# The expert loop of a mixture-of-experts layer, written as a pipeline over blocks

## What is computed

```python
scores = sigmoid(u @ router_w); _, idx = top_k(scores + router_b, 8)      # 128 experts
wts = s_sel / sum(s_sel) * 2.5
# the 4096 (token, expert) pairs, sorted by expert, cut in blocks of one expert each
def group_fn(xg, e):                     # xg: the rows of one block
    g, up = split(xg @ w_gu[e], 2)       # w_gu[e]: 1024 x 512, 2 MB
    return (silu(g) * up) @ w_down[e]    # w_down[e]: 256 x 1024, 1 MB
out = zeros.at[row_tok].add(y * row_w)   # each row is added to its token's sum
```

## Time and profile before

| | us |
|---|---|
| three runs | 1600.34, 1602.52, 1602.64 |
| median | 1602.52 |
| the profiled execution, span from its first to its last instruction | 1598.8 |
| first silu of the expert loop to its last (70 of them) | 742.3 to 1555.5 |

### The profile page before, as it was taken

The page is one execution under the profiler, slowest core; times in us unless marked ns, Lnnn a source line. Parts: engine busy times, 40 slices in busy tenths (PEclk is TensorE's granted clock), DMA queues, the critical chain, the costliest instruction groups (busy, mean ns, idle before and its releaser), DMA issues.

```text
span 1598.8 us, 26750 instructions
## 1 busy us (share of the span) xinstructions
PE 1357.2 (85%) x5742; PEld 975.4 (61%) x5743; DVE 939.1 (59%) x1838; ACT 635.9 (40%) x878; POOL 247.8 (15%) x311
## 2 busy tenths in 40 slices
PE   1699996779999978866989999898899998898990
PEld 0288874568888757534656666666566666565660
DVE  4713338968225876535776576776757556455544
ACT  1363225333213312224555354564555454334432
POOL 0000000000000000002222322323223223232320
PEclk9999998889999989887999999999999999999995
DMA  9412201133225856136999888998989888778743
GB/s 304 133 53 87 72 0 53 53 118 117 94 93 189 284 161 210 66 145 222 329 308 270 243 266 244 329 330 255 315 268 320 243 268 237 213 224 228 218 89 118
DMA packets 111191, 310.59 MB, mean 194 GB/s; under 512 B 16217, under 2 KB 19489, under 8 KB 110898
## 3 DMA queue, kind: packets, MB, share of 16 engines
q1 hardware_dynamic: 82176, 241.20, 43.8%
q0 software_dynamic: 20592, 54.03, 16.1%
q10 hardware_dynamic: 8386, 14.89, 2.6%
...
...
## 4 chain that ended last, share of the span: by engine, by line
PE 42%; DMA 22%; DVE 14%; issue 8%; ACT 6%; ACTq 4%; DVEq 2%; POOLq 1%; POOL 1%; SPq 0%
PE psum L1300 23%; DMA expert_sum<-y_rows,add_idx 12%; PE psum L1467 6%; PE psum L1484 4%; DMA xg<-u_rows,row_idx 4%; DMA gu_raw<-in_exp_w_gu 4%; PE psum L1275 4%; ACT gu_hi L800 2%; DVE tmp_tok L964 2%; ACT y_rows L823 1%; DVE gu_lo L1215 1%; PE psum L1367 1%; PE psum L1358 1%; POOL step_word L547 1%; PE psum L1474 1%
## 5 line engine op out<-in xcount | busy, mean ns | idle before, releaser
L1215 DVE TENSOR_TENSOR gu_lo<-gu_raw,gu_hi 128x1024 f32 x212 | 246.8, 1221 | 112.6 <-ACT gu_hi L800 112.4
L1484 PE MATMUL psum<-w_dn,mask 128*128 x560 | 260.4, 608 | 36.9 <-DVE mask L1235 36.9
L800 ACT ACTIVATE gu_hi<-gu_raw 128x1024 f32 x212 | 209.8, 1048 | 112.7 <-issue 76.4
L1467 PE MATMUL psum<-gu_hi,xT_hi 128*128 x560 | 240.6, 430 | 8.8 <-DVE xT_lo L1205 5.0
L1467 PE MATMUL psum<-gu_hi,xT_lo 128*128 x560 | 219.7, 392 | 0.0
L1467 PE MATMUL psum<-gu_lo,xT_hi 128*128 x560 | 219.1, 391 | 0.0
L1484 PEld LDWEIGHTS psum<-w_dn,mask 128*128 128x128 f32 x560 | 101.2, 190 | 144.6 <-issue 144.6
L400 DVE TENSOR_TENSOR w_lo<-ring,w_hi 128x1024 fp32r<-128x1024 f32 x80 | 95.2, 1223 | 94.5 <-ACT w_hi L393 92.4
L1300 PE MATMUL psum<-uT_hi,w_hi 128*128 128x512 f32 x352 | 138.7, 394 | 13.3 <-DVE w_lo L400 12.2
L823 ACT ACTIVATE y_rows<-psum,row_w 128x512 f32<-128x512 f32 x140 | 88.5, 682 | 147.2 <-DMA expert_sum<-y_rows,add_idx 140.9
L1467 PEld LDWEIGHTS psum<-gu_hi,xT_hi 128*128 128x128 f32 x560 | 105.7, 189 | 56.0 <-issue 36.2
...
## 6 DMA issues: line engine op xcount, KB each, us to landing
...
mods<-in_x ACTq DMA_DIRECT2D x1, 2048.0 KB, 13.0
```

Of the source, the lines that this page charges most:

```text
L800: act.activation(gu_hi[:, bass.ds(order % 2, 1), PK * p:PK * p + PK].rearrange("p o k f -> p (o k) f"), gu_raw[:, PK * p:PK * p + PK], ACT ...
L1215: tt(gu_lo[at].rearrange("p o k f -> p (o k) f"), gu_raw[:, PK * p:PK * p + PK], gu_hi[at].rearrange("p o k f -> p (o k) f").bitcast(F32), ...
L1467: mm = pe.matmul(moe_bank(GU), rows[:, k], w[:, gu_place, k].rearrange("p o n -> p (o n)"), start=(k == 0 and n == 0), stop=(k == KT - 1 a ...
L1484: mm = pe.matmul(moe_bank(Y0 + g), hT[:, j], w_dn[:, place, j, g * NC:(g + 1) * NC].rearrange("p o n -> p (o n)"), start=(j == 0), stop=(j ...
```

## The change

The loop body now holds four blocks. PE makes gate/up of block `b+1` before down of block `b`; down weights and `hT` are split in two parts like the others, so down is twelve `fp32r` matmuls in place of four float32 ones. The three weight tiles hold a whole expert: `ew_raw` (one place), `ew_hi` and `ew_lo` (two places), each loaded and split in three pieces of 1 MB (two of gate/up, one of down). `xT_hi`, `xT_lo` and `y_rows` have two places each, `xg` has two instead of three. A gather is issued three blocks ahead instead of two. ACT may write `y_rows` of `b` once the addition of `b-2` has landed; the additions themselves are still one at a time. The pick is one comparison over 512 columns with `rel` worked out first, instead of four over 128. Ahead of the loop POOL stores the empty row block to the sum twice instead of once.

```diff
-UNROLL, SPAN = 3, 6
+UNROLL, SPAN = 4, 4
+AHEAD = 3
+HALVES = 3
...
             # SP, for each fresh block
-                    for p in range(PIECES):
-                        if not first:
-                            sp.wait_ge(gu_split, order * PIECES + p + 1)
-                        sp.dma_start(gu_raw[:, PK * p:PK * p + PK], ...).then_inc(gu_in[p], 16)
-                load_gu(b + UNROLL)
-                load_down(b + UNROLL, s, 2 * b + 4)
+                    for p in range(HALVES):
+                        sp.wait_ge(ew_split, order * HALVES + p + 1)
+                        sp.dma_start(ew_raw_of(p), ew_source(e, p)).then_inc(ew_in[p], 16)
...
             # POOL, block b
-                pool.wait_ge(xT_psum, 2 * b + 2)
-                gather(b + 2, (s + 2) % UNROLL, 2 * b + 2)
-                pool.wait_ge(scattered, 16 * b + 16)
-                pool.wait_ge(y_ready, 2 * b + 4)
+                pool.wait_ge(xT_psum, b + 2)
+                gather(b + AHEAD, (s + AHEAD) % UNROLL, 2 * b + 3)
+                pool.wait_ge(scattered, 16 * b + 32)
+                pool.wait_ge(y_ready, b + 2)
...
             # ACT, block b (after)
+                act.wait_ge(hT_psum, b + 1)
+                act.activation(hT_hi[:]..., moe_bank(HT)[:, 0:2 * P], ACT.Copy).then_inc(hT_hi_ready, 1)
+                rows_hi(b + 2, s)
+                expert_hi(b + 1, (2,))
+                expert_hi(b + 2, (0,))
+                silu(b + 1)
+                expert_hi(b + 2, (1,))
+                act.wait_ge(idx_ready, b + 1)
+                act.wait_ge(scattered, 16 * b + 16)
+                act.wait_ge(y_psum, b + 1)
+                act.activation(y_rows[:, s % 2], psum[:, Y0:Y0 + 2, :]..., ACT.Copy, scale=row_w[:, s:s + 1]).then_inc(y_ready, 1)
...
             # DVE, block b (after)
+                dve.wait_ge(hT_hi_ready, b + 1)
+                tt(hT_lo[:]..., moe_bank(HT)[:, 0:2 * P], hT_hi[:]..., ALU.subtract).then_inc(hT_ready, 1)
+                dve.wait_ge(y_ready, b + 1)
+                find_rows(b + AHEAD, (s + AHEAD) % UNROLL)
+                dve.wait_ge(scattered, 16 * b + 16)
+                dve.tensor_copy(add_idx[:, s % 2], row_idx[:, s]).then_inc(add_ready, 1)
+                rows_lo(b + 2, s)
+                pick_rows(b + AHEAD + 1)
+                expert_lo(b + 1, (2,))
+                expert_lo(b + 2, (0,))
+                gated_up(b + 1)
+                expert_lo(b + 2, (1,))
...
             # PE, block b (after)
+                pe.wait_ge(h_ready, b + 1)
+                for j in range(2):
+                    mm = pe.transpose(moe_bank(HT)[:, j * P:(j + 1) * P], h_tok[:, bass.ds(j, P, 2)], ident[:])
+                mm.then_inc(hT_psum, 1)
+                find(b + AHEAD)
+                turn_rows(b + 2, s, 16 * (2 * i + (s + 2) // 2) + 16)
+                gate_up(b + 1, s + 1, after)
+                pe.wait_ge(hT_ready, b + 1)
+                pe.wait_ge(ew_split, order * HALVES + 2 * HALVES)
+                pe.wait_ge(y_ready, b + 1)
+                for g in range(2):
+                    for j in range(2):
+                        for m, (w, rows) in enumerate(((ew_hi, hT_hi), (ew_lo, hT_hi), (ew_hi, hT_lo))):
+                            mm = pe.matmul(moe_bank(Y0 + g), rows[:, j], dn_of(w, order, j, g), ...)
```

279 lines of the change are left out of this document (138 added, 141 removed).

## The result

| | us |
|---|---|
| the changed kernel, four runs | 1668.60, 1673.68, 1676.13, 1681.05, median 1674.91 |
| the kernel before on the same chip, median of four runs | 1602.30 |
| ratio, 95% interval | 1.045 [1.042, 1.048] |
| span of the profiled execution | 1671.8 (before 1598.8) |

The forecast was 1568 with a range up to 1606. The change costs 73 us where I expected a gain of 34.

The account below looks back on a forecast made before the run. PE's chain was taken to bound the kernel, DMA right behind. 36 intervals at 12.0 and 33 at 10.2 make 768.6 against 813.2; with +9.9 head and tail, span 1564.1, plus 3.7: 1568 us, 8-in-10 range 1530 to 1606.

Parts of the forecast that it names:

- The clock: PE's clock in the loop falling where PE idles 2 us a block: named as a way to be wrong, no price.
- 12.0: Forecast interval in us for the 36 fresh-to-fresh blocks, set by the loads' cycle; 11.79 a block before.
- PE idle ahead of gate/up for the last split: Sign in the loop that the order fails; called already contained in the fresh intervals, 12.0 against PE's 9.8.
- Register loads: Loads and tests before each DVE split, three times a block: taken as nothing, at most one uncovered stretch of 1.8 us.
- Gathers: Two-block loop through down, ACT, DVE, POOL and gate/up: 19.5 us with landing 6.4; 10.2 taken for the 33 other intervals.
- Loads: One raw place per 1 MB weight piece: landing 7.6, cycle 12.25 us with high and low parts; 12.0 taken.
- DVE's sum: DVE's work in a fresh block, three splits included: 10.9 us, 11.2 with gaps, above PE's 9.8.
- Additions: POOL's chain of landing, step and issue in the loop: 10.3 us a block at the median, hidden in the forecast.
- the second rival: Additions bind the loop: chain 12.9 us in fresh stretches, 10.9 elsewhere; time 1623, chance 0.13.
- Head and tail: Outside the loop: second store to the sum +3.2 us, dead block's find, turns and gate/up +6.7; together +9.9.
- PE's own work: PE's work per block in the loop (gate/up, down, turns, find): 9.8 us.
- the third: Rival that the gain goes back: loads 12.5, gathers at their longest landing 10.7 us; time 1602.3, chance 0.12.

Follow-up runs that it names:

- e13_filler12: The changed kernel with 12 transposes of a constant on PE before it waits for the split, filling its idle time; 1691.8 us.
- e15_no_piecewise: e12_raw_twice with PE again waiting for both gate/up pieces before its first matmul; 1547.7 us, against 1533.2.
- e3_hoist: The changed kernel with ACT and DVE loading the words fresh and order once at the head of a block, not before each split; 1657.0 us.
- e6_whole_piecewise: The changed kernel with down weights in one part and PE waiting for the second gate/up piece only before gate/up's second half; 1733.5 us.
- e5 to e8: Four changed kernels: down weights whole; also piecewise gate/up wait; also register loads once a block; split weights with both: 1720.3, 1733.5, 1703.7, 1660.8 us.
- e1_piecewise: The changed kernel with PE waiting for the second gate/up piece's split only before the second half of gate/up; 1674.9 us.
- e12_raw_twice: The changed kernel with gathers four ahead, down weights whole, piecewise gate/up wait, register loads once a block, two raw gate/up places; 1533.2 us.

## Why the prediction was wrong

*Two steps failed: PE's clock, which I put at nothing, and the chain, which is in no sum of mine.* By the intervals of the changed kernel the first is the larger.

*The clock.* My forecast had PE idle 2.2 us in a fresh block (12.0 against 9.8). I named the clock as what would make me wrong and gave it no price and no chance, because it showed 1.00 in both windows of the kernel before, where PE idles 1.2 us a fresh block. The changed kernel idles 2.0, and 36 gate/ups of the loop, 31 of them in fresh-to-fresh intervals, run at half clock: at 1.59 each, 57 us of the 108. This is a count over the trace, not a saving that a run shows: e13_filler12 brings the clock back and loses the gain to the gather loop.

*The chain.* I compared sums for each engine and a cycle for each place (DVE 11.2, PE 9.8, load 12.25) and took the largest. 12.0 came out for the fresh intervals, and the bare chain measures 11.88, but that is luck: the chain is none of those sums. I never followed what an interval depends on through ACT's written order, silu ahead of the high part of piece 1, and then through PE's wait for both pieces. The text even dismissed it ("PE idle ahead of gate/up for the last split; in the fresh intervals the sum has that already"). The sum did not have it: the chain needs no load and binds also where loads are early. So the intervals behind a second block, which I had at 10.2 with DVE light and loads early, cannot fall below 11.88: 27 of their 36 us, and most of the rest is the clock. e15_no_piecewise shows the chain by putting back its one link.

*Register loads.* Taken as nothing, because a running split would cover them on DVE. The uncovered ones are on ACT, behind a silu that is short and that ACT had waited for: 1.16 us inside the chain, the difference of 1.47 and 0.31 from silu to high part in the changed kernel and in e3_hoist. My own bound for one uncovered stretch on DVE, 1.8, was of that size.

*Gathers.* The mechanism and the terms were right, two sizes were off: 6.4 for a landing that is 7.6 in the loop, 8.6 in the all-fresh stretch from 1027 to 1149 and 9.4 in e6_whole_piecewise, and no half clock behind the wait. It did not show in the changed kernel's common interval, since the chain was longer; it made a part of its late intervals (such as 1528.3 to 1545.6, where PE waits 5.19 us for a gather) and ate what e5 to e8 freed.

*Loads.* The 1 MB gate/up pieces land in 6.1 us, not 7.6; in that all-fresh stretch 7.3. The Trainium skill (DMA: Bandwidth & Descriptors, Bandwidth) has 6.15 for 1 MB, counted without the issue; by the row it was the better figure. Piece 1, the one that counts, takes 6.6 in the median of the fresh-to-fresh intervals, but 8.2 to 8.6 in most of that stretch: 8.4 + 1.92 + 2.29 + 0.6 of hand-overs and issue is 13.2, a second loop just under the chain. ACT's waits for loads went up to 82 us in e1_piecewise, and two raw places brought -9 us in e12_raw_twice.

*DVE's sum.* 2.29 a split and 1.22 for `xT_lo`, as put down. In the same stretch it is busy 10.4 of 13.6 us.

*Additions.* Hidden, as said, and the second rival did not come about in the changed kernel. POOL's step takes 0.77 us in the mean, 0.18 at the least and 1.27 in the median beside a split, so the lengthening that the rival counts on is there, but POOL mostly waits for `y_rows` and not for a landing. In e12_raw_twice, where the rest is out of the way, the additions do set the fresh stretches.

*Head and tail.* +2.0 for +3.2, and +14.4 for +6.7. The tail holds the dead block's gate/up at 9.5 us after the last live one; the rest of it I did not follow up.

*PE's own work.* Right: 9.52 in the intervals that nothing else holds, for 9.8.

None of the rivals was this one. The second has the nearest time, 1623, by a mechanism that stayed hidden; the third has the nearest idea, a gain that goes back, and stops at 1602.
